# A two-block transformer on one core: the next weight tile by token tile at three norms, low parts of some splits on GpSimd, and GLA's last gate tile in parts

## The reference, cut to what matters

```python
for l in range(2):
    mix = diff_moba_mixer(...) if l == 0 else gla_mixer(...)
    x = layer_norm(ALPHA * x + mix, ln_mix_g[l], ln_mix_b[l])
    x = layer_norm(ALPHA * x + square(relu(x @ w1[l])) @ w2[l], ln_ffn_g[l], ln_ffn_b[l])
# gla_mixer: q, k, v, r, low = split(x @ w_in)      (512, 512, 1024, 1024, 16 columns)
#   g = log_sigmoid(low @ w_gate_up + b) / 16;  o = gla(q, k, v, g)   (4 heads)
#   return (rms_norm(o) * silu(r)) @ w_out
```

## Time and profile before

| | before |
|---|---|
| three runs, us | 1716.16, 1716.29, 1713.0; median 1716.16 |
| profiled execution, us | 1713.44, span 1711.6 |
| mean granted clock | 0.94 |
| busy PE, DVE, ACT, POOL | 81%, 66%, 32%, 27% |
| ffn(0), ffn(1) on PE | about 1182 to 1363, 1523 to 1703 |

### The profile page before, as it was taken

The page is one execution under the profiler, slowest core; times in us unless marked ns, Lnnn a source line. Parts: engine busy times, 40 slices in busy tenths (PEclk is TensorE's granted clock), DMA queues, the critical chain, the costliest instruction groups (busy, mean ns, idle before and its releaser), DMA issues.

```text
span 1711.6 us, 17345 instructions
## 1 busy us (share of the span) xinstructions
PE 1380.6 (81%) x6264; PEld 971.9 (57%) x6264; DVE 1131.3 (66%) x2051; ACT 539.2 (32%) x1023; POOL 454.7 (27%) x393
## 2 busy tenths in 40 slices
PE   6976788777777677777777788658999899789998
PEld 5875668523223232222222267547999687679996
DVE  6655665688887788886555556647756659577564
ACT  2453434222221213212111233323434246234341
POOL 1154305244443443544444200000211025001110
PEclk9988899999998999999999989878999999889999
DMA  9554526799999999999999823204555534245550
GB/s 367 190 184 148 196 74 227 293 421 409 421 421 412 421 408 382 400 422 420 422 421 421 344 75 123 98 25 142 182 196 197 189 110 147 75 151 179 188 197 25
DMA packets 116629, 433.17 MB, mean 253 GB/s; under 512 B 6832, under 2 KB 7088, under 8 KB 83520
## 3 DMA queue, kind: packets, MB, share of 16 engines
q0 software_dynamic: 36864, 268.45, 38.0%
q1 hardware_dynamic: 79392, 162.51, 26.8%
q10 hardware_dynamic: 288, 1.11, 0.2%
HBM read 431.00 MB, written 1.05 MB: 252 GB/s over the span
## 4 chain that ended last, share of the span: by engine, by line
PE 47%; DMA 23%; DVE 19%; ACT 6%; issue 2%; POOL 2%; SPq 0%; DVEq 0%; ACTq 0%; POOLq 0%
PE PS L45 45%; DMA EB<-in_experts,EI 22%; DVE EB L78 5%; DVE WL L75 3%; ACT BIG L24 2%; PE PS L84 1%; DVE X L63 1%; POOL W L75 1%; ACT WH L24 1%; DVE Y L75 1%; DMA W<-in_w_ada 1%; DVE GV L75 1%; DVE EB L63 1%; DVE XL L75 1%; DVE ST L69 1%
## 5 line engine op out<-in xcount | busy, mean ns | idle before, releaser
L45 PE MATMUL PS<-EB,BIG 128*128 128x512 f32 x1024 | 495.4, 628 | 169.9 <-ACT BIG L24 169.8
L45 PEld LDWEIGHTS PS<-EB,BIG 128*128 128x128 f32 x1024 | 190.3, 197 | 470.3 <-ACT BIG L24 287.3
L78 DVE CUSTOM_DVE_ANT_0 EB<-EB,Y 128x1024 f32<-128x1024 f32 x256 | 313.4, 1224 | 146.0 <-DMA EB<-in_experts,EI 145.0
L39 POOL DMA_INDIRECT EB<-in_experts,EI x256 | 288.3, 1126 | 397.0 <-PE PS L45 380.9
L75 DVE TENSOR_TENSOR WL<-W,WH 128x1024 fp32r<-128x1024 f32 x228 | 297.5, 1351 | 109.5 <-ACT WH L24 109.3
L45 PE MATMUL PS<-XH,WH 128*128 128x256 f32 x928 | 272.0, 293 | 12.8 <-DVE WL L75 10.0
L24 ACT ACTIVATE WH<-W 128x1024 fp32r<-128x1024 f32 x240 | 237.8, 1047 | 91.8 <-PE PS L45 84.9
L45 PE MATMUL PS<-XL,WH 128*128 128x256 f32 x928 | 265.0, 286 | 0.0
L45 PE MATMUL PS<-XH,WL 128*128 128x256 f32 x928 | 265.0, 286 | 0.0
L45 PEld LDWEIGHTS PS<-XH,WH 128*128 128x128 f32 x928 | 180.9, 195 | 17.9 <-DVE WL L75 11.1
L45 PEld LDWEIGHTS PS<-XL,WH 128*128 128x128 f32 x928 | 180.8, 195 | 2.7 <-issue 2.4
(11 more groups left out here) (170 smaller groups left out, 1512.1 us busy)
## 6 DMA issues: line engine op xcount, KB each, us to landing
W<-in_ffn_w SPq DMA_DIRECT2D x32, 2048.0 KB, 8.8
W<-in_w_ada SPq DMA_DIRECT2D x12, 2048.0 KB, 12.2
W<-in_w_in SPq DMA_DIRECT2D x6, 2048.0 KB, 12.9
W<-in_hy_w_in SPq DMA_DIRECT2D x6, 2048.0 KB, 13.5
W<-in_gla_w_in SPq DMA_DIRECT2D x6, 2048.0 KB, 7.9
W<-in_w_query SPq DMA_DIRECT2D x4, 2048.0 KB, 8.2
W<-in_w_out SPq DMA_DIRECT2D x2, 2048.0 KB, 8.3
EB<-in_experts,EI POOLq DMA_INDIRECT x256, 11.1
```

The source lines that it names most:

```text
L39: return lambda e: e.indirect_dma_start(*a, **k)
L45: return lambda e: e.matmul(*a, **k)
L78: return lambda e: e.tensor_tensor_reduce(*a, **k)
```

## The change

At the three norms that are followed by a weight tile of which both halves can be had token by token (mixer 0 to ffn(0), ffn(0) to GLA, mixer 1 to ffn(1)), the next tile is computed token-major by `both_tiles`: token tile 0, then the turn of X's token tile 1, then token tile 1. What comes out is transposed later (`turn_tokens`, `turn_query`). In GLA the value tiles come before the gate tiles, the first step of `levels()` stands ahead of the query's transposes, and the last gate half is three groups of blocks (0 to 2, 3 and 4, 5 to 7) between the last level's steps and the heads. The low parts of ten tiles are computed on GpSimd.

```diff
+        def both_tiles(tile, before, evac=lambda t, b, tk: None):
+            done = []
+            for t in range(2):
+                if t:
+                    before.last()
+                b = bank()
+                tk = dense(PS[b][:, :], take(tile), tm_pairs(tile, t), before.xt[t], *bank_free[b])
+                if t:
+                    wdone(tile, tk)
+                done.append(evac(t, b, tk))
+                tick(2)
+            return done
...
+        on_pool = [*hy_out, *(ffn_tiles[0][0][0, j] for j in range(2)), gla_in[0], gla_in[1], gla_in[5], *gla_out,
+                   *(ffn_tiles[1][0][0, j] for j in range(2))]
         for t in tiles[hyt[2].index:]:
-            later_split(t)
+            later_split(t, pool if t in on_pool else None)
...
+            def square_tokens(t, b, tk):
+                r = Y[:, 0, t * 512:(t + 1) * 512]
+                td = dve(lambda e: e.tensor_scalar(r, PS[b][:, :], 0.0, None, ALU.max), tk, *at_free[0])
+                bank_free[b] = (td,)
+                return r, act(lambda e: e.activation(r, r, ACT.Square), td)
+
+            def turn_tokens(t):
+                r, ta = squares[t]
+                ts = slice(t * 128, (t + 1) * 128)
+                b = bank()
+                for c in range(4):
+                    tk = tr(PS[b][:, c * 128:(c + 1) * 128], r[:, c * 128:(c + 1) * 128], ta, *bank_free[b])
+                hi, lo = (a[:, 0, 0:4, ts] for a in (AH, AL))
+                ps = PS[b][:, :].rearrange("p (c t) -> p c t", c=4)
+                th = act(lambda e: e.activation(hi, ps, ACT.Copy), tk, *at_free[0], ordered=False)
+                tl = dve(lambda e: e.tensor_tensor(lo, ps, hi.bitcast(F32), ALU.subtract), th, ordered=False)
...
+            squares = both_tiles(up[0, 0], before, square_tokens)
...
-                        fm_tile(up[g, j], ev, *t_xt)
+                        fm_tile(up[g, j], ev, *t_xt, hook=turn_next)
...
+        def evac_query(t, b, tk):
+            ta = act(lambda e: e.activation(QT2[:, t, :], PS[b][:, :], ACT.Copy, scale=128.0 ** -0.5), tk, ordered=False)
...
+        t_query = both_tiles(gla_in[0], norm, evac_query)
+        t_xt = norm.tokens
         b = bank()
         tk = narrow(b, wg_parts[0], *t_xt)
         ta = act(lambda e: e.activation(GL, PS[b][0:16, 0:256], ACT.Copy), tk)
...
-        fm_tile(gla_in[0], evac_flat(0, 128.0 ** -0.5), *t_xt)
         t_bg2 = gate_sums()
-        fm_tile(gla_in[1], evac_flat(1024, 1.0))
+        lv = levels()
+        next(lv)
+        for t in range(2):
+            e_free[0] = e_free[1] = (turn_query(t),)
+            tick(2)
+        fm_tile(gla_in[1], evac_flat(1024, 1.0), *t_xt)
         t_qk = act.last
-        lv = levels()
         next(lv)
...
         for j in range(2):
-            tm_tile(gla_in[4 + j], with_levels(evac_silu(j)), n=2)
-        for j in range(2):
             tm_tile(gla_in[2 + j], with_levels(evac_tok(lambda t: VG[:, t, j * 512:(j + 1) * 512])), n=2)
+        t_v = (act.last, dve.last)
+        tm_tile(gla_in[4], with_levels(evac_silu(0)), n=2)
+        last_gate = take(gla_in[5])
+        b = bank()
+        tk = dense(PS[b][:, :], last_gate, tm_pairs(last_gate, 0), *bank_free[b])
+        bank_free[b] = with_levels(evac_silu(1))(b, 0, tk)
+        t_sg = [pool.last]
+        tick(2)
...
+        gate_part(range(0, 3))
+        next(lv)
+        gate_part(range(3, 5))
         for _ in lv:
             pass
...
+        tk_gate = gate_part(range(5, 8))
...
+        ready = head_norm(0, head_squares(0))
+        t_square = head_squares(1)
+        bank_free[b_gate] = evac_silu(1)(b_gate, 1, tk_gate)
+        after.pop()()
+        t_sg.append(pool.last)
+        x_heads = [turn_tile(Y[:, 0, :], 0, ready)]
+        ready = head_norm(1, t_square)
...
+        for t in range(2):
+            for j in range(2):
+                b = 4 + 2 * t + j
+                tk = dense(PS[b][:, :], take(gla_out[j]), tm_pairs(gla_out[j], t), x_heads[t], *bank_free[b],
+                           mid=norm_mix.mid if (j, t) == (1, 1) else None)
...
+                if (j, t) == (1, 0):
+                    x_heads.append(turn_tile(Y[:, 1, :], 1, ready))
+                norm_mix.give(j, b, t, tk, turn=False)
+                if (j, t) != (1, 1):
+                    tick(2)
```

More of the change, by code:

```diff
@@ L233, in build @@
         turn = [0]
+        filling = set()
         def bank():
+            while turn[0] % 4 in filling:
+                turn[0] += 1
             b = turn[0] % 4
@@ L322, in build @@
         ffn_tiles = [plan_ffn(0)]
-        gla_in = {j: wplan_on(A["gla_w_in_2"], 0, j) for j in (0, 1, 4, 5, 2, 3)}
+        gla_in = {j: wplan_on(A["gla_w_in_2"], 0, j) for j in range(6)}
         gla_out = [wplan_on(A["gla_w_out_2"], 0, j) for j in range(2)]
@@ L559, in close_pair @@
                         wdone(pair[j], tk)
-                    norm.give(j, b, t, tk)
+                    norm.give(j, b, t, tk, turn=False)
                     if (j, t) != (1, 1):
                         tick(n)
+        def both_tiles(tile, before, evac=lambda t, b, tk: None):
[10 more added lines that the diff above has]
+            return done
         def log_exp_tables():
@@ L1646, in layer_norm, with ffn @@
             return Normed(piece, stats, apply, X, turned=not last)
-        def ffn(l, t_xt, norm, beside=None):
+        def ffn(l, before, norm, beside=None):
             up, down = ffn_tiles[l]
@@ L1651, in ffn, with turn_next @@
             y_free = [() for _ in range(4)]
-            turns = [0]
-            at_ready = {}
+            turns = [2]
+            at_ready, at_first = {}, []
+            def square_tokens(t, b, tk):
[13 more added lines that the diff above has]
+                tl = dve(lambda e: e.tensor_tensor(lo, ps, hi.bitcast(F32), ALU.subtract), th, ordered=False)
+                bank_free[b] = (tl,)
+                y_free[t] = (tk,)
+                at_first.append(tl)
+            squares = both_tiles(up[0, 0], before, square_tokens)
+            t_xt = before.tokens
+            turning = [0, 1]
+            def turn_next():
+                if turning:
+                    turn_tokens(turning.pop(0))
             for g in range(5):
@@ L1656, in ffn @@
                     for j in range(2):
+                        if (g, j) == (0, 0):
+                            continue
                         def ev(b, c, tk):
@@ L1678, in ffn @@
                         tk = dense(PS[b][:, :], tile, tm_pairs(tile, t, AH[:, q % 2, :, :], AL[:, q % 2, :, :]),
-                                   *at_ready[q], *bank_free[b], start=(q == 0), stop=(q == 3),
+                                   *at_ready[q], *at_first, *bank_free[b], start=(q == 0), stop=(q == 3),
                                    mid=norm.mid if q == 3 and i == 3 else None)
@@ L1691, in close_mixer @@
             close_pair(pair, norm, *t_xt)
-            return norm.tokens
-        t_xt = close_mixer(0, hy_out, t_xt)
+            return norm
+        norm_mix = close_mixer(0, hy_out, t_xt)
         f = (pe.last, dve.last, act.last)
@@ L1701, in build @@
         norm = layer_norm(A["ln_ffn_g_2"][0], A["ln_ffn_b_2"][0])
-        ffn(0, t_xt, norm, beside=lambda free: wg_parts.append(narrow_parts(wg, 16, 0, t_wg, *free)))
-        t_xt = norm.tokens
+        ffn(0, norm_mix, norm, beside=lambda free: wg_parts.append(narrow_parts(wg, 16, 0, t_wg, *free)))
         f = (dve.last, act.last)
@@ L1713, in build @@
         GL = GVf[0:16, 2816:3072]
+        QT2 = BIG[:, 3072:4096].rearrange("p (t c) -> p t c", t=2)
+        def evac_query(t, b, tk):
+            ta = act(lambda e: e.activation(QT2[:, t, :], PS[b][:, :], ACT.Copy, scale=128.0 ** -0.5), tk, ordered=False)
+            bank_free[b] = (ta,)
+            return ta
+        t_query = both_tiles(gla_in[0], norm, evac_query)
+        t_xt = norm.tokens
         b = bank()
@@ L1717, in build, with turn_query @@
         bank_free[b] = (ta,)
+        def turn_query(t):
+            b = bank()
+            for c in range(4):
+                tk = tr(PS[b][:, c * 128:(c + 1) * 128], QT2[:, t, c * 128:(c + 1) * 128], t_query[t], *bank_free[b])
+            ta = act(lambda e: e.activation(QG.rearrange("p (h t) -> p h t", h=4)[:, :, t * 128:(t + 1) * 128],
+                                            PS[b][:, :].rearrange("p (h t) -> p h t", h=4), ACT.Copy), tk, ordered=False)
+            bank_free[b] = (ta,)
+            return tk
         ZG, LG = Y[:, 0, :], Y[:, 1, :]
@@ L1857, in build, with gate_part @@
         for j in range(2):
-            tm_tile(gla_in[4 + j], with_levels(evac_silu(j)), n=2)
-        for j in range(2):
             tm_tile(gla_in[2 + j], with_levels(evac_tok(lambda t: VG[:, t, j * 512:(j + 1) * 512])), n=2)
+        t_v = (act.last, dve.last)
+        tm_tile(gla_in[4], with_levels(evac_silu(0)), n=2)
+        last_gate = take(gla_in[5])
+        b = bank()
```

(42 more changed lines are left out.)

6 lines of the change are left out of this document (4 added, 2 removed).

## The result

The changed kernel takes 1736.24 us (median; 1734.46 to 1738.13) against 1716.22 us (1713.0 to 1717.26) of the kernel before beside it: ratio 1.012, 95% interval 1.0102 to 1.0138. The forecast was 1712.9, range 1703 to 1720. Time and sign were wrong. The profiled execution took 1735.3 us, span 1733.5, mean granted clock 0.932: 21.9 us above that of before.

A forecast was written before the change was run, and what follows sets the result against it. TensorE was taken as the bound, other work counting only where it waits. Terms of -2.8, +4.3, -8.2 and +3.4 summed to -3.3 us: 1710.1 for the profiled execution, 1712.9 for the median, range 1703 to 1720.

The forecast's parts named there:

- A: Norm before ffn(0): token tile 0 of the next tile fills TensorE's wait at the norm; -2.8 us.
- C: GLA from the diagonal products to the end of the mixer: shorter waits, 101.9 us instead of 110.1; -8.2 us.
- D: Norm before ffn(1): as A, but TensorE stalls 5.1 us for late GpSimd pieces of up[0, 1]; +3.4 us.
- GpSimd splits cost nothing here: Norm before ffn(0): up[0, 1]'s last two GpSimd pieces end near Z + 13, long before 18.8, so add no time.
- B: Norm before GLA to the diagonal products: level 0's Exp holds ScalarE's queue, TensorE waits 8.8 us; +4.3 us.
- R3: Rival: in GLA, GpSimd's queue falls behind as its prices stretch beside VectorE; +4.7 us, 1720.9; chance 0.18.
- R1: Rival: the clock holds at TensorE's restarts, keeping five at 1.9 us; -12.8 us, 1703.4; chance 0.12.
- R2: Rival: no TensorE wait at t_qk before the diagonal products; -14.0 us, 1702.2; chance 0.13.
- R4: Rival: no change that can be told, A and C each half as large; +2 us, at most 1718; chance 0.14.

The follow-up runs named there:

- one-tensor steps: Changed kernel with the layer norms' three small square-root steps as tensor_scalar with a pointer scalar, reading one tensor each: 1716.43 us, ratio 1.0014.
- all on VectorE: Changed kernel with all low parts back on VectorE, new order of the work kept: 1713.22 us, ratio 0.9998.

## Why the prediction was wrong

The step that failed is in term A, and C and D leaned on it: **"GpSimd splits cost nothing here"**, with DVE's chain at calm price. I priced GpSimd's pieces by GpSimd's own queue and DVE's steps by rows in which GpSimd was idle. Nowhere did I ask what a norm on DVE costs while GpSimd runs. The pieces of the next tiles are made during the close, so they lie beside the norm of token tile 0, whose `mid` turn had 2.5 us to spare at the calm price of 5.8 us (1158.19 to 1164.0, wanted at 1166.5); 7.7 us of holds used that up.

The terms can be checked one by one from PE's timelines, between the ends of the closes' last matmuls (Z) and the start of the diagonal products. C ends at the Z of mixer 1's close; D goes from there to the first partial sum of ffn(1)'s close on DVE. Differences to before, us:

| term | predicted | changed kernel | one-tensor steps | all on VectorE |
|---|---|---|---|---|
| close of mixer 0, up to Z | 0 | +5.6 | -0.6 | -4.9 |
| A, Z to Z of ffn(0)'s close | -2.8 | +4.1 | -2.0 | 0.0 |
| B, Z to diagonal products | +4.3 | +1.0 | +2.6 | +5.1 |
| C, to Z of mixer 1's close | -8.2 | +4.6 | -2.4 | -5.5 |
| D, to ffn(1)'s close | +3.4 | +6.5 | +4.7 | +1.4 |
| sum | -3.3 | +21.9 | +2.4 | -3.8 |

The sum in the last column is of one execution; by the medians that kernel stands at 0.9998. What varies from run to run lies above all in the first line, which has the first 1160 us in it.

- **A.** Its queue was right to a tenth: counted from 1177.43, where token tile 0 starts, token tile 1 started at 11.2 (predicted 11.3) and ended at 18.9 (18.8). The ReLU, Square, WH, XH, XL order on ACT was as written. With the `mid` hold gone A is -2.0. In the changed kernel the hold at ffn(0)'s close (5.27) and its clock (1.6) lie in A; without them it is -2.7. The other two lie in the first line and in C. In the last column A lacks the 1.3 that XL waits behind DVE's own split pair, and 5.2 are lost at the turn instead of 4.5.
- **B.** Right in kind, too large in two places. The Exp did hold ACT's queue, PE did wait at `t_qk`, 5.86 and not 8.8, for the six WH pieces that follow the Exp on ACT at 1406.26 and 1408.63. The restart behind the norm's 3.34 kept the clock, which I had charged with 1.9. Moving the step took 7.7 us off the median: the wait of 5.9 becomes 0.7, and the restart's half clock goes with it.
- **C.** The largest term was mis-sized. The waits that I named are there: DVE's before level 7's products 4.60 (2.4 predicted, 2.00 without GpSimd), the head turn's 3.06 (about 3), the second's 1.57. But 5.8 of the 8.2 are missing even with the `mid` hold gone. By the first head turn 5.2 of them are lost (with one-tensor steps it comes 79.4 us behind the start of the diagonal products, against 51.5 + 9.5 + 11.3 and 1.9 of clock in the sum): 2.2 on level 7's wait, 1.4 on half clock in its products (3.22 for 16 instead of 1.8). The other 1.6 was not followed up. The longer wait at level 7 is a hold too: level 7's two operands on DVE take 4.02 us beside GpSimd's pieces, 1.42 in the kernel without them, and the difference of 2.6 is that between the waits of 4.60 and 2.00:

```profile
1472.16 4.02 DVE L75 TENSOR_TENSOR Y<-BIG,Y 128x512 f32<-128x512 f32 x2
```

```profile
1472.84 5.56 POOL L75 TENSOR_TENSOR WL<-W,WH 128x1024 fp32r<-128x1024 f32 x2
```

- **D.** Its waits were right: PE waited 3.41 and 1.63 for GpSimd's pieces of `up[0, 1]`, predicted 3.4 and 1.7; on DVE the stall was 2.4, predicted 2.7. It came out 1.8 larger in the changed kernel than with one-tensor steps, and that is the clock: behind the wait for XL the first 12 matmuls take 5.28 against 4.17, and in the 20 us behind PE's second wait for GpSimd it is busy throughout in both, at 0.85 (first row, the changed kernel) against 0.88, worth 0.6:

```profile
1555.70:1575.70 20.00, 20.00 (x147) 20.00 (x148) 12.18 (x13) 9.38 (x12) 2.60 (x2) 0.85 0.30 104
```

```profile
1537.02:1557.02 20.00, 20.00 (x153) 20.00 (x154) 12.79 (x13) 9.93 (x12) 2.58 (x2) 0.88 0.30 106
```

- **R3** named the right two engines with the wrong form and place. It let prices stretch by a ratio and asked whether GpSimd's queue gets through GLA (44 us in 51.5). The cost is a hold for each DVE instruction with two SBUF tensors, whatever its size, and its place was the three norms. Therefore 1720.9 was too low. The section "Who interferes with whom" of "SBUF — State Buffer" in the Trainium skill, which I did not draw on, has the form: a VectorE instruction with two SBUF inputs contends with a GpSimd instruction that reads SBUF, and the contention for the port pair that the two engines share is an exclusive lock. The traces here agree (2.19 us for a 128x1 step beside pieces of 2.35, 1.08 beside pieces half as long).
- **R1** did not happen: in the changed kernel the clock was at 0.50 behind each wait of 4.5 or more, fell to 0.50 within 1.5 us of the restart behind the head turn's 3.06, and was 1.00 behind the norm's 3.34 and the second head turn's 1.57. **R2** did not either. **R4** is, by its size, what the order alone gives.

What stays open: where the other 1.6 that C lost before the head turn lies, and what makes the clock fall behind one wait of 2.5 and not behind another. Neither was tried.

## What to carry to other kernels

Before moving elementwise work to GpSimd, list the VectorE instructions with two SBUF operands that will run beside it, on the path that PE waits for: price each at one whole GpSimd instruction, even if it has one column. If such work must lie there, give the small steps one tensor and a scalar pointer, or cut GpSimd's instructions short. And when a tile is computed in halves to cover a turn, emit the turn ahead of the splits and of every evacuation that waits for another engine: three such moves of a few lines made 24 us here (1713.22 to 1689.56).

## What the runs showed of the hardware

- VectorE's 128x1 tensor_tensor, 0.16 us alone, took 2.19 us beside GpSimd pieces of 128x1024 and 1.08 beside pieces of 128x512.
- A 128x1 operand given as a tensor_scalar's scalar pointer does not count as a second tensor: 0.24 us a step beside the same GpSimd pieces, and 0.24 without them.
- VectorE instructions that read PSUM and one SBUF tensor were not held (a 128x512 scalar_tensor_tensor took 0.69 us beside GpSimd pieces and without them).
- The hold goes both ways: GpSimd's piece took 2.35 us beside small steps and 2.96 beside VectorE's split pair.
